# Three weight chunks of each layer fetched once in float32 and split on the chip: a two-layer encoder kernel on one Trainium2 core

## What is computed

```
h = rms_norm(x, g);  z = h @ w_in            # 1024 -> 3712
aq ak av ag | bq bk bv bg | ca cb cg = split(z)
ya = neighbourhood_attention(aq, ak, av) * silu(ag)   # 4 heads
yb = dilated_attention(rope(bq), rope(bk), bv) * silu(bg)   # 6 heads
yc = (silu(layer_norm(conv31(ca * sigmoid(cb)))) @ w_pw + b_pw) * silu(cg)
x  = x + concat(ya, yb, yc) @ w_out
```

## Time and profile before

| what | value |
|---|---|
| median of 3 runs | 513.06 us (511.6 to 513.33) |
| the profiled execution | 513.21 us, of it the span of the instructions 511.4 us |
| PE busy | 501.6 us (98% of the span) |
| DVE, ACT, POOL busy | 365.1, 275.5, 164.0 us |
| moved by DMA | 97.79 MB, mean 191 GB/s |

### The profile page before, as it was taken

One profiled execution on the slowest core, in us unless ns is written; L12 is line 12 of the kernel. 1 busy time (PEld: TensorE's weight loads), 2 busy tenths in 40 slices (PEclk: granted clock), 3 DMA queues, 4 the chain that ended last, 5 costly groups with the idle time before them and its releaser, 6 DMA issues.

```text
span 511.4 us, 10279 instructions
## 1 busy us (share of the span) xinstructions
PE 501.6 (98%) x3998; PEld 401.9 (79%) x3998; DVE 365.1 (71%) x741; ACT 275.5 (54%) x531; POOL 164.0 (32%) x224
## 2 busy tenths in 40 slices
PE   8999999999999999999999999999999999999995
PEld 6888877887777778788888887878787877778883
DVE  6999978899984666521539878887999656852424
ACT  6844667664664475524425447676646646752314
POOL 0013332221143557425411333222122355663101
PEclk9999999999999999999999999999999999999998
DMA  8715889669986997999502378975999979899964
GB/s 292 308 43 132 198 210 207 132 162 204 232 215 159 236 251 168 245 237 278 159 2 82 88 163 196 214 174 102 220 219 223 226 166 266 217 243 247 203 169 164
DMA packets 55120, 97.79 MB, mean 191 GB/s; under 512 B 19872, under 2 KB 33696, under 8 KB 55072
## 3 DMA queue, kind: packets, MB, share of 16 engines
q0 software_dynamic: 19648, 62.93, 54.3%
q1 hardware_dynamic: 35136, 34.02, 23.1%
q10 hardware_dynamic: 288, 0.19, 0.1%
HBM read 84.92 MB, written 5.90 MB: 178 GB/s over the span
## 4 chain that ended last, share of the span: by engine, by line
PE 93%; DMA 4%; issue 1%; ACT 0%; DVE 0%; POOL 0%; POOLq 0%; SPq 0%; ACTq 0%; DVEq 0%
PE acc L607 22%; PE acc L608 21%; PE acc L609 21%; PE sc L718 5%; PE tp L751 4%; DMA w_lo<-w_out 3%; PE misc L782 2%; PE sc L669 2%; PE sc L607 1%; PE sc L609 1%; PE sc L608 1%; PE sc L670 1%; PE sc L671 1%; PE misc L777 1%; PE acc L647 1%
## 5 line engine op out<-in xcount | busy, mean ns | idle before, releaser
L607 PE MATMUL acc<-act_hi,w_hi 128*128 128x512 f32 x480 | 194.5, 405 | 0.1
L608 PE MATMUL acc<-act_hi,w_lo 128*128 128x512 f32 x480 | 187.7, 391 | 0.0
L609 PE MATMUL acc<-act_lo,w_hi 128*128 128x512 f32 x480 | 187.1, 390 | 0.0
L607 PEld LDWEIGHTS acc<-act_hi,w_hi 128*128 128x128 f32 x480 | 90.2, 188 | 21.9 <-issue 3.9
L609 PEld LDWEIGHTS acc<-act_lo,w_hi 128*128 128x128 f32 x480 | 90.2, 188 | 19.9
L608 PEld LDWEIGHTS acc<-act_hi,w_lo 128*128 128x128 f32 x480 | 90.3, 188 | 17.1 <-issue 0.5
L877 ACT ACTIVATE w_lo<-w_hi 128x1024 fp32r<-128x1024 f32 (+1 forms) x62 | 61.9, 999 | 47.3 <-DMA w_hi<-w_out 38.0
L1320 DVE SCALAR_TENSOR_TENSOR y<-ub,par,y 128x512 f32<-128x512 f32 x90 | 70.0, 777 | 0.0
L1092 POOL DMA_DIRECT2D w_lo<-w_in x40 | 35.9, 897 | 106.2 <-ACT w_lo L877 105.5
L1320 DVE SCALAR_TENSOR_TENSOR ub<-ub,par 128x512 f32<-128x512 f32 x84 | 63.3, 754 | 0.0
L939 ACT ACTIVATE prob<-prob,nmx 128x384 f32<-128x384 f32 (+1 forms) x80 | 45.3, 567 | 25.1 <-DVE nmx L1342 24.9
(11 more groups left out here) (150 smaller groups left out, 718.7 us busy)
## 6 DMA issues: line engine op xcount, KB each, us to landing
w_hi<-w_in POOLq DMA_DIRECT2D x40, 512.0 KB, 5.8
w_lo<-w_in POOLq DMA_DIRECT2D x40, 512.0 KB, 6.1
w_hi<-w_out POOLq DMA_DIRECT2D x16, 512.0 KB, 6.4
w_lo<-w_out POOLq DMA_DIRECT2D x16, 512.0 KB, 7.0
pT<-w_in SPq DMA_DIRECT2D x15, 512.0 KB, 5.5
v<-v_way SPq DMA_DIRECT2D x40, 112.0 KB, 5.3
v_way<-vs SPq DMA_DIRECT2D x24, 112.0 KB, 5.6
gf<-nabias SPq DMA_DIRECT2D x20, 128.0 KB, 5.5
```

What stands on the lines that cost most here:

```text
L607: nc.tensor.matmul(to[:, :], w_hi[:, slot, k, :], a_hi[:, k, :], start=i == 0, stop=False)
L608: nc.tensor.matmul(to[:, :], w_lo[:, slot, k, :], a_hi[:, k, :], start=False, stop=False)
L609: last = nc.tensor.matmul(to[:, :], w_hi[:, slot, k, :], a_lo[:, k, :], start=False, stop=i == K - 1)
```

## The change

The chunks 27, 28 (of `w_in`) and 32 (of `w_out`) of each layer leave POOL's two transfers. SP fetches each once, as float32, into `v_far`, seen as 128x1024. ACT copies it rounded to `w_hi`, DVE subtracts to give `w_lo`. Slots: the loads stand on SP in slots 27, 31, 35, the copies on ACT in 29, 33, 38, the subtractions on DVE in 30, 34, 39. Each load waits until DVE has done the chunk before it, since all three share one buffer.

```diff
+LATE = (27, 28, 32)
+LATE_LOADS = {27: 27, 31: 28, 35: 32}
+LATE_HI = {29: 27, 33: 28, 38: 32}
+LATE_LO = {30: 27, 34: 28, 39: 32}
+def by_transfers(c):
+    return not by_engines(c) and c not in LATE
...
+        raw_late = v_far[:, :, :, :].rearrange("p g i t -> p (g i t)").rearrange("p (k t) -> p k t", t=P)
...
+            def load_late(l, c):
+                if c == LATE[0]:
+                    sp.wait_ge(pv_done, PAIRS * l + DPAIRS)
+                if nth_late(l, c) > 1:
+                    sp.wait_ge(late_lo, nth_late(l, c) - 1)
+                sp.dma_start(raw_late, chunk_src(l, c)[0]).then_inc(late_in, 16)
...
                     if DUNITS + 2 <= n < DUNITS + 2 + BIASES - BIAS_RING:
                         load_bias(l, n - DUNITS - 2 + BIAS_RING)
+                    if n in LATE_LOADS:
+                        load_late(l, LATE_LOADS[n])
                     if n in V_STORES:
                         store_v(l, V_STORES[n])
...
+                elif c in LATE:
+                    pe.wait_ge(late_lo, nth_late(l, c))
                 else:
                     pe.wait_ge(wlo_in[(N_CH * l + c) % SPL], landed(l, c))
...
+            def late_split(l, c):
+                act.wait_ge(tile_done, N_CH * l + c - SPL + 1)
+                act.wait_ge(late_in, 16 * nth_late(l, c))
+                nc.scalar.activation(w_hi[:, c % SPL, :, :], raw_late, ACT.Copy).then_inc(late_hi, 1)
...
                         norm(l, n - 1)
+                    if n in LATE_HI:
+                        late_split(l, LATE_HI[n])
                     if n < UNITS:
                         if n % 2 == 0:
                             split_next(l, tile_at(n)[0])
...
             def hi_next(l, c):
                 f = follows(l, c + CAST_AHEAD)
-                if f is not None and not by_engines(f[1]):
+                if f is not None and by_transfers(f[1]):
                     load_hi(*f)
...
+            def late_rest(l, c):
+                dve.wait_ge(late_hi, nth_late(l, c))
+                nc.vector.tensor_tensor(w_lo[:, c % SPL, :, :], raw_late, w_hi[:, c % SPL, :, :], ALU.subtract)\
+                    .then_inc(late_lo, 1)
```

More of the change, by code:

```diff
@@ L228, in build @@
         cleared = sem("cleared")
+        late_in = sem("late_in")
+        late_hi = sem("late_hi")
+        late_lo = sem("late_lo")
         hi_ready = sem("hi_ready")
@@ L307, in landed, with nth_late @@
         def landed(l, c):
-            return 16 * sum(not by_engines(d % N_CH) for d in range(c % SPL, N_CH * l + c + 1, SPL))
+            return 16 * sum(by_transfers(d % N_CH) for d in range(c % SPL, N_CH * l + c + 1, SPL))
         def nth(l, c):
-            return sum(by_engines(d % N_CH) == by_engines(c) for d in range(N_CH * l + c + 1))
+            return sum(by_engines(d % N_CH) == by_engines(c) and d % N_CH not in LATE for d in range(N_CH * l + c + 1))
+        def nth_late(l, c):
+            return len(LATE) * l + LATE.index(c) + 1
         def nth_split(l, c):
@@ L507, in load_v @@
                     sp.wait_ge(pv_done, PAIRS * l + max(g - 1, 0))
+                if l and g == 0:
+                    sp.wait_ge(late_lo, len(LATE) * l)
                 for j in range(QUADS):
@@ L666, in row_products @@
                     if a == 0 and i % 2 == 0:
-                        pe.wait_ge(wlo_in[slot], landed(LAST, c))
+                        if c in LATE:
+                            pe.wait_ge(late_lo, nth_late(LAST, c))
+                        else:
+                            pe.wait_ge(wlo_in[slot], landed(LAST, c))
                     to, rows, k = ROW_BANKS[half][a], slice(a * P, (a + 1) * P), K_ORDER[i]
@@ L886, in split_hi @@
                 nc.scalar.activation(w_hi[:, c % SPL, :, :], raw[:, m % RAW, :, :], ACT.Copy).then_inc(hi_ready, 1)
+            def late_split(l, c):
+                act.wait_ge(tile_done, N_CH * l + c - SPL + 1)
+                act.wait_ge(late_in, 16 * nth_late(l, c))
+                nc.scalar.activation(w_hi[:, c % SPL, :, :], raw_late, ACT.Copy).then_inc(late_hi, 1)
             def split_next(l, c):
                 f = follows(l, c + AHEAD)
-                if f is not None and (f[0] or f[1] >= EARLY):
+                if f is not None and f[1] not in LATE and (f[0] or f[1] >= EARLY):
                     (split_hi if by_engines(f[1]) else negate)(*f)
@@ L1539, in _ @@
                                                     ALU.add).then_inc(hn_ready, 1)
+                    if n in LATE_LO:
+                        late_rest(l, LATE_LO[n])
                     if n > UNITS:
```

## The result

The changed kernel takes 515.41 us (median of 6 executions, 514.72 to 515.89) against 513.07 us for the kernel before in the same comparison: a ratio of 1.0052, 95% interval 1.0037 to 1.0068. It is slower by 2.3 us. The forecast was 511.7 us.

A forecast was written before the change was run, and what follows sets the result against it. PE was taken as the bound, with only its gaps to gain. The profiled 513.21 us less 0.97, 0.30 and 0.15 gave 511.8, forecast as a median of 511.7 us, range 510.7 to 514.6.

The forecast's parts named there:

- So only PE's gaps can be given back: Whole kernel: PE busy 501.6 of 511.4 us, other engines far from full; its three gaps, 1.59 us, are the most to gain.
- 0.97 before chunk 32 in the last layer: PE's 1.20 us step into chunk 32, waiting for its second `w_out` transfer, loses its excess: gain 0.97 us.
- 0.30 and 0.15 in the first layer: PE's gains: 0.30 us before chunk 32, and 0.15 (bounds 0 and 0.32) before `values` of pair 4.
- Rival B: Chunk 28's load on SP lands late, delaying `values` of pair 3 in each layer; up to 515.3 us; chance 0.17.
- The fit that the prediction quotes: Chunk 28's load: 2.0 us plus bytes over 436 GB/s gives 3.2 us for 512 KB; prediction took 5.5 from the trace.
- Rival C: Last layer: PE's wait moves to chunk 33, leaving about 0.5 of 1.27 us gained, time 512.6 us; chance 0.13.
- DVE's wait for `store_v` of pair 4: DVE's `vs<-prob` of unit 32 waits some 0.6 us longer in last layer, about 3 in first, without affecting PE.

The follow-up runs named there:

- e5: Only chunk 32 changed against the kernel before, its load in SP's slot 27; 27 and 28 stay on POOL: 516.63 us, ratio 1.0067.
- e12: Kernel before with chunk 32 alone changed, plus a DRAIN on POOL between the two layers: 515.73 us (one execution).
- e14: Kernel before with chunk 32 alone changed and POOL's closing DRAIN left out: 512.07 us, ratio 0.9965.
- e11: The changed kernel (all three chunks) with POOL's closing DRAIN left out: 512.97 us, ratio 0.9999.
- e1: The changed kernel with 12 small transfers added on POOL after its last weight transfer, 180 in all: 516.76 us, ratio 1.008.
- e7: The changed kernel with 12 small transfers added at the start of POOL's program: 515.99 us (one execution).
- e2: The changed kernel with 12 memsets added at POOL's end and no more transfers: 515.76 us, ratio 1.0065.
- e8: The changed kernel with 28 small transfers added at the start of POOL's program: 514.93 us (one execution).

## Why the prediction was wrong

**The step that failed** is the first: "So only PE's gaps can be given back". With it the sum took all that lies behind PE's last matmul as fixed. It is fixed for ACT, DVE and SP, whose closing rows all moved by the same 1.3 us, but not for POOL. Its closing DRAIN goes by 0.0815 us for each of its own transfers in the record, was covered by 0.4 us in the kernel before, and went from 4.01 to 7.57 us, by the count from 41 transfers to 85. Of the 3.56 us, 3.13 are on the path. That POOL would issue fewer transfers stood in the prediction as a relief; this DRAIN got longer with fewer, and that could not have been worked out from the trace of before. That the cover was 0.4 us thick could have been: it stands in the rows of the closing line.

**0.97 before chunk 32 in the last layer**: right. It measured 0.96 by the step, and from the end of the first layer's attention part (`values` of pair 4) to the last matmul PE took 286.38 us in place of 287.38.

**0.30 and 0.15 in the first layer**: wrong, they measured nothing. The step into chunk 32 went, but 0.21 came back inside the chunk, where PE now arrives before DVE has finished the activations, and 0.14 before `values` of pair 4, whose last move landed 0.29 us earlier (216.64 against 216.93) where PE came 0.42 earlier. From a matmul in the feed of both kernels (154.97 before, 154.55 after) to that place PE took 62.26 us before and 62.40 after. With chunk 32 alone more than the first layer's gain is lost before `values` of pair 4: the step there is 1.22, 1.29 and 1.23 us in e5, e12 and e14, against 0.47 to 0.64 in the four profiled executions of the kernel before. PE comes there 0.7 to 1.0 us earlier than in the kernel before, but POOL's last move lands at 216.5 to 216.9, hardly earlier than the 216.93. The remaining 0.42 of the 1.28 us lies in the part of the program that the change does not touch, so these rows put 0.86 to the change.

**Rival B** (the load of chunk 28 lands late): its mechanism is absent. That load was issued at 427.25 and ACT could copy it at 432.27, 5.0 us, where 5.5 was taken; SP's moves started 0.9 us later than before, where up to 1.5 was expected. This is the line of SP's new loads:

```profile
L513 SPq DMA_DIRECT2D v_far<-w_in x4: 327/330/334, 160.7 to 427.3; - x4
L513 SPq DMA_DIRECT2D v_far<-w_out x2: 430/430/430, 189.9 to 437.0; - x2
...
DMA to landing us min/median/max: 3.5/4.8/7.1
```

The fit that the prediction quotes for this load is given in the Trainium skill for transfers that GpSimd issues, and the load is SP's; the six loads took 3.5 to 7.1 us, and nothing in the sum rested on the fit. The place of B was right in other executions, by another mechanism: the moves themselves land later, I take it since the load of chunk 32, issued ahead of them, shares the 16 DMA engines with them. The Trainium skill (DMA: Bandwidth & Descriptors, Issuing engines are not separate DMA queues) gives that rule, and the moves in e11 (3.8 to 6.0 against 2.9 to 3.8 us) agree with it. The price was put on the load of chunk 28; it fell on the small moves behind that of chunk 32.

**Rival C** (the wait moves to chunk 33): absent. PE's step there is 0.23 us in both layers of the kernel after.

**DVE's wait for `store_v` of pair 4**: half right. `vs<-prob` of unit 32 waits 1.05 us in place of 0.66, but starts 1.0 us earlier (433.11 against 434.12), since the bias tile ahead of it no longer keeps DVE waiting for 1.76 us. In the first layer it waits 0.84 us, where it did not wait before and some 3 us were expected; it starts 1.5 us later there (184.20 against 182.72), and in this execution PE's `values` of pair 3 follow by 0.31 us all the same.

```profile
184.20 0.45 DVE L1396 STREAM_TRANSPOSE vs<-prob 128x256 f32<-128x256 f32 x1 [0.84 <-DMA v_way<-vs]
...
433.11 0.45 DVE L1396 STREAM_TRANSPOSE vs<-prob 128x256 f32<-128x256 f32 x1 [1.05 <-DMA v_way<-vs]
```

What stays open: what shortens POOL's record, and so why the change at these chunks left about 85 transfers in it at the end and not 41. It hangs neither on the total of transfers (e1, e7) nor on the time at which POOL ends (the DRAIN of e2, e7, e8 and the kernel after is the same within 2 ns while its start moves from 505.3 to 506.3).

## What to carry to other kernels

Read the closing line of every engine before calling the tail fixed: when each engine's DRAIN starts, how long it takes, and which ended last. An engine that issues many transfers itself can have a closing DRAIN of 4 to 9 us, as here, and where it is hidden by only a few tenths of a microsecond, a change to that engine's transfers can bring it out. A DRAIN where the engine is idle anyway, or none, took it off the end here; whether a kernel may do without the closing one for good these runs don't show. And of a change that pays in one place and adds traffic in two others, try the paying part alone: here chunk 32 alone, without the closing DRAIN, is the version that is faster (0.9965). Chunk 32 alone with a DRAIN in POOL's idle time was not run.

## What the runs showed of the hardware

- GpSimd's closing DRAIN took 0.65 us where GpSimd had issued no transfer since another DRAIN, 7.85 us with 88 transfers since, and 0.0815 us more for each small transfer added at the end, but for one step of 36 transfers: 4.0 to 9.4 us at the end of these kernels. Size does not matter much: 2 KB transfers cost what the mixture of 512 KB and small ones costs (e1, e12). The DRAINs of DVE, ACT, SP and PE in the same place took 0.79, 0.73, 0.01 and 4.27 us in both kernels.
- The Trainium skill (VectorE: DVE Perf Modes, The DRAIN you can't avoid) says that the boilerplate DRAINs of preamble and postamble are about 12 ns on all five engines. At the start of the program the rows are near that (7 to 10 ns in both kernels, but 186 and 187 on GpSimd). At its end only SyncE's is. The closing DRAIN of GpSimd can be left out by an option of the kernel's block, so these may not be the DRAINs that the page means; no run tells.
- Fewer transfers can make GpSimd's closing DRAIN longer: 180 gave 4.0 us, 168 gave 7.6, 172 gave 9.3 and 176 gave 9.4.
